# Expert input table loaded in pairs of chunks: 1 MB per transfer, 8 KB per partition, ring of two pairs

## The reference

```python
def peer_ffn(h, w_q, sub_keys, u_tab, v_tab):
    q = (h @ w_q).reshape(B, S, PEER_HEADS, 2, PEER_DQ // 2)
    scores = jnp.einsum('bshpd,hpkd->bshpk', q, sub_keys)
    ...                       # top 16 of 128 keys twice, top 16 of their 256 sums: ids, gate
    def block(args):
        hx, idx, g = args
        u = u_tab[idx]
        act = jax.nn.gelu(jnp.einsum('thkd,td->thk', u, hx))
        return jnp.einsum('thk,thkd->td', g * act, v_tab[idx])
```

## Time and profile before

| | |
|---|---|
| median of 3 executions | 2917.0 us (2916.68 to 2919.65) |
| the profiled execution | 2919.88 us, of which the span of the trace is 2918.2 us |
| PE busy | 2496.7 us, 86% of the span |
| DVE busy | 1903.4 us, 65% |
| ACT busy | 1211.0 us, 41% |
| POOL busy | 329.4 us, 11% |
| loads of the input table (L1868) | 256, of 512 KB each |
| stage of the change, first layer | from 1012.0 to about 1443 us of the span |
| stage of the change, second layer | from 2114.6 to about 2545 us of the span |

### The profile page before, as it was taken

How to read it: one execution, slowest core, us unless ns; L and a number is a source line. 1 busy time by engine, 2 the same in 40 slices (tenths; PEclk the granted TensorE clock), 3 DMA queues, 4 the chain that set the end, 5 groups by cost and what they waited for, 6 DMA issues and landing times. The chain is left out here.

```text
span 2918.2 us, 45550 instructions
## 1 busy us (share of the span) xinstructions
PE 2496.7 (86%) x15092; PEld 2080.9 (71%) x15092; DVE 1903.4 (65%) x3341; ACT 1211.0 (41%) x1859; POOL 329.4 (11%) x297
## 2 busy tenths in 40 slices
PE   6986996598696799998899996745899999899997
PEld 6634844295244799998788885732799998788886
DVE  5553674255864478878766675456488879867665
ACT  4321423043321244565544553342244565544444
POOL 0000000000310000000033353000000000034332
PEclk9887997799897899999999998867899999999999
DMA  6332551444351377664477775422277674377775
GB/s 184 125 115 91 154 171 60 137 174 145 130 185 69 107 223 228 219 216 145 143 243 241 239 242 159 142 64 84 73 231 229 217 226 151 131 241 241 242 240 176
DMA packets 289402, 498.23 MB, mean 171 GB/s; under 512 B 81417, under 2 KB 157449, under 8 KB 289313
## 3 DMA queue, kind: packets, MB, share of 16 engines
q1 hardware_dynamic: 264816, 494.88, 53.2%
q10 hardware_dynamic: 24496, 2.19, 0.7%
HBM read 462.35 MB, written 34.65 MB: 170 GB/s over the span
## 5 line engine op out<-in xcount | busy, mean ns | idle before, releaser
L2177 PE MATMUL psum<-split_operands 128*128 128x512 f32 x3072 | 702.1, 391 | 13.5 <-ACT split_operands L2135 13.5
L2177 PEld LDWEIGHTS psum<-split_operands 128*128 128x128 f32 x3072 | 580.2, 189 | 134.9 <-ACT split_operands L2135 13.9
L1897 PE MATMUL psum<-split_operands 128*128 128x256 f32 x4096 | 542.5, 286 | 19.1 <-ACT split_operands L1932 19.0
L1897 PEld LDWEIGHTS psum<-split_operands 128*128 128x128 f32 x4096 | 511.4, 193 | 23.2 <-DVE split_operands L2015 16.0
L2148 DVE TENSOR_TENSOR split_operands<-weights_ring,split_operands 128x1024 fp32r<-128x1024 f32 x256 | 315.6, 1233 | 215.7 <-ACT split_operands L2135 215.7
L2122 POOL TENSOR_TENSOR arena<-arena,residual_gates 128x256 f32 (+1 forms) x256 | 273.4, 1068 | 1280.8 <-DMA residual_gates<-expert_activations 1280.8
L2135 ACT CAST split_operands<-weights_ring 128x1024 fp32r<-128x1024 f32 x256 | 269.4, 1052 | 350.8 <-PE psum L2177 347.7
L1975 DVE TENSOR_TENSOR split_operands<-weights_ring,split_operands 128x1024 fp32r<-128x1024 f32 x256 | 313.1, 1223 | 108.8 <-ACT split_operands L1932 108.3
L255 PE MATMUL psum<-split_operands 128*128 128x256 f32 x2304 | 291.3, 291 | 40.6 <-DVE split_operands L278 40.6
L255 PEld LDWEIGHTS psum<-split_operands 128*128 128x128 f32 x2304 | 290.0, 200 | 42.8 <-DVE split_operands L285 42.7
L1901 PE MATMUL psum<-split_operands 128*128 128x256 f32 x2048 | 288.2, 283 | 0.0
(11 more groups left out here) (304 smaller groups left out, 2435.5 us busy)
## 6 DMA issues: line engine op xcount, KB each, us to landing
weights_ring<-in_peer_u_dram SPq DMA_DIRECT2D x256, 512.0 KB, 3.7
weights_ring<-in_peer_v_dram SPq DMA_DIRECT2D x256, 512.0 KB, 4.5
weights_ring<-in_w_ada_dram SPq DMA_DIRECT2D x48, 1024.0 KB, 5.1
expert_activations<-residual_gates SPq DMA_DIRECT2D x256, 128.0 KB, 2.0
residual_gates<-expert_activations SPq DMA_DIRECT2D x256, 128.0 KB, 4.2
weights_ring<-in_w_in_dram SPq DMA_DIRECT2D x6, 2048.0 KB, 8.0
weights_ring<-in_hg_w_in_dram SPq DMA_DIRECT2D x5, 2048.0 KB, 8.1
arena<-in_hg_w_in_dram SPq DMA_DIRECT2D x5, 2048.0 KB, 8.0
```

The lines of the kernel that those rows point to most:

```text
L1897: nc.tensor.matmul(K.ps[:, 4 + b, 0:SEQ], u_t[:, b, 0, k], h[:, wh, k], start=(k == 0 and wh == 0), stop=False)
L2177: last = nc.tensor.matmul(K.ps[:, 4 + 2 * t + half], g[:, s, w, t * P:(t + 1) * P], vs[:, b, wv, half * 512:(half + 1) * 512], start=(star ...
```

## The change

Two consecutive chunks become one transfer. On the host the table is laid out as 64 pairs, each with 8 KB in one piece per partition (chunk 2m first, then chunk 2m + 1). SP loads pair m into slots 2s and 2s + 1 with s = m % 2. The ring in SBUF has the same size, now seen as two pairs. A pair's load waits until both chunks of the pair before the last one are free (`ut_low` at 2m - 2), and then both stores of that older pair follow it. There is one load semaphore per pair of slots; ACT's wait before the cast of an odd chunk asks for the same load as that of the even one. Nothing else in the stage is changed.

```diff
-        u_loaded = [sem(f"u_loaded{n}") for n in range(SLOTS)]
+        u_loaded = [sem(f"u_loaded{n}") for n in range(2)]
...
-            def load(n, s, early):
+            def load(m, s, early):
                 if not early:
-                    sp.wait_ge(ut_low, n - (SLOTS - 1))
-                sp.dma_start(u[:, s].rearrange("p k e -> p (k e)"),
-                             table[bass.ds(n, 1)].rearrange("a p k e -> p (a k e)")).then_inc(u_loaded[s], 16)
+                    sp.wait_ge(ut_low, 2 * m - 2)
+                sp.dma_start(u[:, 2 * s:2 * s + 2].rearrange("p c k e -> p (c k e)"),
+                             table[bass.ds(m, 1)].rearrange("a p c k e -> p (a c k e)")).then_inc(u_loaded[s], 16)
                 if not early:
-                    store(n - SLOTS, s)
+                    for c in range(2):
+                        store(2 * m - SLOTS + c, 2 * s + c)
...
-            pipeline(sp, 0, NKEYS, SLOTS, load)
+            pipeline(sp, 0, NKEYS // 2, 2, load)
...
-                act.wait_ge(u_loaded[s], slot_loads(n, s))
+                act.wait_ge(u_loaded[s // 2], slot_loads(n, s))
...
-    inputs["peer_u_2"] = u.transpose(0, 2, 4, 3, 1)
+    inputs["peer_u_2"] = u.transpose(0, 2, 4, 3, 1).reshape(DEPTH, NKEYS // 2, 2, P, KD, NKEYS).transpose(
+        0, 1, 3, 2, 4, 5)
```

## The result

| | kernel before | changed kernel |
|---|---|---|
| median of 20 executions each | 2918.63 us (2911.65 to 2923.96) | 2925.03 us (2922.02 to 2928.84) |
| ratio | | 1.0022, 95% interval 1.0015 to 1.0028 |
| span of the profiled execution | 2918.2 us | 2925.8 us |

The changed kernel is slower by 6.4 us (4.4 to 8.2 by the interval). The forecast was 3.9 us more, 2920.9 us, with a range to 2925.0. The median lies just above that range, and the loss is 1.6 times the one forecast. The median of 20 executions of the kernel before is itself 1.6 us above that of the three that were known. As a difference, 6.4 us is less than the 8.0 us that the range allowed above 2917.0, so it is this higher base that carries the median over the end of the range.

The account below looks back on a forecast made before the run. The prediction took PE to bound the kernel until 1297 us and DVE the last 32 chunks, DMA only the start. Terms of 1.46, 1.41, 0.5 and 0.5 us made 3.9 on 2917.0: 2920.9 us, range 2915.5 to 2925.0.

Parts of the forecast that it names:

- the landing of the first pair: At each layer's stage start: the pair lands 5.2 us after issue, making the first cast 1.46 and 1.41 us later.
- the clock behind it: PE's granted clock during chunk 0's matmuls: up to 0.8 us per layer either way, taken as 0.
- the landing at the hand-over: Load of chunks 96 and 97: landing of 5.0 us against a distance of 4.5, slipping the cast by 0.5 us.
- the start: First cast of each layer's stage, waiting for its whole pair: 2.9 us in both layers, bounds 2.3 and 3.8.
- the hand-over: Passage to the gate matmuls at chunk 96, where DVE waits for the cast: 1.0 us together, bounds 0 and 2.2.
- the steady part: Chunks between start and gates: pair loads land in 5.0 us, within the 6.3 us distance less 0.2; cost 0.
- the routing part: Around chunks 75 to 78: shortest distance from release to cast is 5.5 us, enough for a 5.0 us landing.
- The stores: On SP behind the pair's load and wait: up to one chunk later, needed some 11 us away; cost 0.
- the coarser wait: Each pair's load waits for the later of two chunks, with over 1 us left in the steady part; cost 0.
- the two-transfer row: At the start, the first two chunks in two transfers: complete 5.6 and 5.7 us after the first issue.
- Rival (a): Pair landing L long enough to count at start and hand-over: 5.8 us lost at L = 5.6; chance 0.22.
- The Trainium skill's figure: Fit for GpSimd-issued transfers, 2.0 us plus bytes over 436 GB/s: start costs 1.3 us, hand-over nothing, 2918.3 in all.

Follow-up runs that it names:

- e3: Changed kernel with each layer's first pair loaded as two 512 KB transfers and chunk 93's subtraction ahead of the gate numbers: 2920.79 us, 0.9993 of the kernel before.
- e4: Changed kernel's waits and SP order, but each pair issued as two 512 KB transfers with own semaphores: 2917.09 us, 0.9988 of the kernel before.
- e1: Changed kernel with only each layer's first pair loaded as two 512 KB transfers, a semaphore each: 2924.19 us, 1.0011 of the kernel before.
- e6: Changed kernel plus 14 identity matmuls on TensorE at the stage start, while it waits: 2924.04 us, 1.0019 of the kernel before.
- e2: Changed kernel with VectorE's subtraction for chunk 93 moved ahead of its wait for the gate numbers and their copies: 2925.58 us, 1.0018 of the kernel before.
- e7: Changed kernel with pair 0 loaded in the stage before and chunk 93's subtraction ahead of the gate numbers: 2918.92 us, 1.0002 of the kernel before.
- e8: Kernel before (single loads) with chunk 0 loaded in the stage before and 9 identity matmuls on TensorE: 2912.86 us, 0.9982 of the kernel before.
- e5: Changed kernel with 1 MB transfers, but the table in DRAM as before, in 4 KB rows: 2925.77 us, 1.0036 of the kernel before.

## Why the prediction fell short

**The two places, and the direction, were right.** What failed is the size of three terms of the sum: the landing of the first pair, the clock behind it, and the landing at the hand-over. The forecast named the start and the hand-over, said that the steady part and the routing part would hide their loads, and that PE's share there would stay. The table of stretches shows just that (0.02 us at most between chunks 10 and 95), and e3 shows that nothing else costs. The stores and the coarser wait were put at 0, and e4 bears that out for the stage. One reading in the prediction was wrong without harm: DVE does have idle time before 1297 (busy 57.73 of 77 us). It is PE, busy all the time there, that has no hole in which a late start could be made up.

**First mis-sized term: the landing of the first pair.** I took 5.2 us, nearer to the 1 MB rows of another stage than to the two transfers with the same bytes in the same place. It was 5.5 and 5.8 us. The reason given for going under the two-transfer row, that the second issue of 0.4 us is saved, was hardly worth anything: 5.6 and 5.7 was nearly the answer. The start cost 1.79 + 2.02 = 3.8 us, not 2.9. This is the upper end that the text had from that row.

**Second: the clock, put at 0.** The text bounded it at 0.8 us either way per layer and took the middle. It came to +0.70 and +0.60. In the kernel before the clock rose 9.4 us after the first issue with PE started at 4.9 to 5.0 us; in the changed one at 12.8 us with PE started at 6.7 to 7.0 us. In e1 and e3, with PE started between 5.2 and 5.4, it was again 9.4 to 9.5. A start later by 1.8 and 2.0 us thus cost 2.5 and 2.6 us. e6 shows that the clock is the cause: with matmuls ahead of chunk 0 and the full clock at its start, the slow chunk is gone. This term is 1.3 us of the 7.2.

**Third: the landing at the hand-over.** Put at 5.0, as the median of single loads plus the difference to the 1 MB rows; it was 5.4 and 5.5, while the median of all pairs is 5.1. With the distance of 4.5 us that rows 10 and 11 had given, and 0.1 us from the landing to the cast, it made 0.98 and 1.15, not 0.5 and 0.5. e2 confirms the mechanism and that the slip reaches the end.

Together: 3.8 + 1.3 + 2.1 = 7.2 us against 2.9 + 0 + 1.0. Rival (a), whose formula 2 x (2L - 8.25) gives 5.7 us at a landing L of 5.55, came nearest. By itself that is still just under the 5.8 us at which this rival begins; with the clock it is 7.0. It had 0.22, and the forecast 0.55. The three errors have one sign: both landings were taken too low, and the clock, taken in the middle of its bounds, cost time in both layers. The one transfer at the edge of a stage and the one at the tightest place were sized mainly by rows of a steady flow, although the two of the kernel before that stood at the very edge were in the profile.

**The Trainium skill's figure.** The fit in "DMA: Bandwidth & Descriptors", section "Anatomy of one DMA — SWDGE (gpsimd) path", is for transfers issued by GpSimd and makes an estimate of 4.4 us for 1 MB, which would have given 1.3 us in all. The runs show 4.9 at the least and 5.1 in the median for the loads issued by SP, so for these the measurement decides against it. The Trainium skill's rule of at least 1 MB per transfer, which the section "Rules for kernel authors" of the same page gives for the most bandwidth, found nothing to gain. DMA had kept ACT waiting for 5.4 us in the kernel before, at the starts alone, and this wait is the one that larger transfers make longer.

## What to carry to other kernels

In this kernel a transfer in the steady stream could be made larger without cost, because its landing fits the distance from the last release to the next use. Look for the shortest such distance chunk by chunk, not in the mean, and above all where the work changes its bound. At the start of a stage the first transfer is best kept small (512 KB and not 1 MB in e1 and e3), or issued in the stage before, where the ring is free (e7, and in e8 together with the identity matmuls). And what delays TensorE's start is paid for more than once when the clock has fallen: 1.8 us of delay were 2.5 us of time.

## What the runs showed of the hardware

- The granted clock did not rise a fixed time after PE's start. PE started 4.9 to 5.4 us after the first issue and had the full clock at 9.3 to 9.6 us (the kernel before, e1, e3, e4); with a start at 6.7 to 7.0 us it had it at 12.7 to 12.8 us (the changed kernel, e2), and in e5 with 6.9 and 7.3 us at 12.0 and 12.8 us. With the identity matmuls of e6 the full clock was there 5.95 us into the stage in the first layer, and never left in the second.
- The time of a 1 MB load from issue to landing, on an otherwise similar stream, was 4.9 us at the least and 5.1 in the median, with 5.5 to 6.1 for the first of a stage (the changed kernel, e2, e5, e6), 5.4 and 5.5 at the hand-over of the changed kernel, and 6.2 there in e6, in both layers alike.
- Rows of 8 KB made packets of 8 KB and no difference in the median landing, 5.1 us with either row.
